# Chunk matrices moved ahead of the last three latent token tiles, and the order of the stores behind them

## The reference, cut to what matters

```python
proj = hn @ w_in                                   # all head groups read columns of it
qkv = silu(causal_depthwise_conv(proj[..., :1536], conv_w))
# gated delta rule, per chunk and head, with the decays of g and beta:
a_low = where(strict, einsum('cd,ed->ce', k_beta, k) * decay, 0)
w = triangular_solve(a_low + eye, k_beta * exp(g));  u = triangular_solve(a_low + eye, v_beta)
# multi-scale pool
o_b = (group_linear(window_means(proj[..., POOL]) - proj[..., POOL])) * pool_scale
# latent attention: q and k from two low-rank latents, normalised per head, rotated
q_c = rotary(rms_norm(rms_norm(proj[..., CQ]) @ w_uq));  kv = rms_norm(proj[..., CKV]) @ w_ukv
x = x + concat[o_a, o_b, o_c] @ w_out
x = x + swiglu(rms_norm(x))
```

## Time and profile before

| | us |
|---|---|
| median of 3 runs | 1263.68 |
| lowest, highest | 1263.26, 1266.42 |
| the profiled execution | 1261.1 |
| its span in the profile | 1259.4 |
| PE busy | 1223.4 (97%) |
| VectorE busy | 826.0 (66%) |
| ScalarE busy | 470.6 (37%) |
| GpSimd busy | 410.7 (33%) |

### The profile page before, as it was taken

One profiled execution on the slowest core, in us unless ns is written; L12 is line 12 of the kernel. 1 busy time (PEld: TensorE's weight loads), 2 busy tenths in 40 slices (PEclk: granted clock), 3 DMA queues, 4 the chain that ended last, 5 costly groups with the idle time before them and its releaser, 6 DMA issues.

```text
span 1259.4 us, 17475 instructions
## 1 busy us (share of the span) xinstructions
PE 1223.4 (97%) x6206; PEld 1022.3 (81%) x6206; DVE 826.0 (66%) x1261; ACT 470.6 (37%) x776; POOL 410.7 (33%) x371
## 2 busy tenths in 40 slices
PE   8999999999798999999999999999999999999998
PEld 7887777887788888888778888888888887888887
DVE  6446777886576676544765656556565589777786
ACT  6312223332334343333544333333333344344342
POOL 6001111441122222102655655665665356100000
PEclk9999999999899999999999999999999999999999
DMA  8311333536732121042325665653667359585544
GB/s 249 119 51 30 113 92 109 164 125 167 251 105 66 56 80 33 1 148 86 119 70 159 206 201 187 214 197 117 201 227 260 92 164 308 174 255 145 175 128 173
DMA packets 190886, 183.17 MB, mean 145 GB/s; under 512 B 19598, under 2 KB 146908, under 8 KB 190812
## 3 DMA queue, kind: packets, MB, share of 16 engines
q1 hardware_dynamic: 190688, 182.16, 45.8%
q10 hardware_dynamic: 124, 0.04, 0.0%
HBM read 124.50 MB, written 56.62 MB: 144 GB/s over the span
## 4 chain that ended last, share of the span: by engine, by line
PE 68%; DVE 17%; issue 5%; POOL 3%; DMA 3%; ACT 3%; SPq 1%; DVEq 0%; ACTq 0%; POOLq 0%
PE ps L2363 30%; PE ps L2368 13%; PE ps L2274 5%; PE ps L2134 5%; PE ps L2010 4%; DVE stage L1594 2%; PE ps L2241 2%; PE ps L2210 1%; PE ps L1986 1%; DVE w_lo L1472 1%; DVE wop_lo L1873 1%; PE ps L2229 1%; DVE stage L1588 1%; POOL mla_sc L964 1%; DVE xop L1857 1%
## 5 line engine op out<-in xcount | busy, mean ns | idle before, releaser
L2363 PE MATMUL ps<-xop,wop_hi 128*128 128x512 f32 x1232 | 379.8, 390 | 1.7 <-ACT snap L1409 0.8
L2363 PEld LDWEIGHTS ps<-xop,wop_hi 128*128 128x128 f32 x1232 | 230.8, 188 | 51.0 <-issue 2.3
L2363 PE MATMUL ps<-xop,wop_lo 128*128 128x512 f32 x616 | 239.7, 389 | 0.0
L2368 PE MATMUL ps<-dop,wop_hi 128*128 128x512 f32 x440 | 136.2, 391 | 2.7 <-DVE x L1955 2.7
L2363 PEld LDWEIGHTS ps<-xop,wop_lo 128*128 128x128 f32 x616 | 115.6, 188 | 24.1
L1873 DVE TENSOR_TENSOR wop_lo<-w_sumS,wop_hi 128x512 fp32r<-128x512 f32 (+1 forms) x104 | 86.7, 836 | 68.6 <-ACT wop_hi L1352 68.6
L1873 DVE TENSOR_TENSOR wop_lo<-w_pair,wop_hi 128x512 fp32r<-128x512 f32 (+1 forms) x76 | 87.4, 1151 | 36.8 <-ACT wop_hi L1352 36.7
L2010 PE MATMUL ps<-act_hi,w_hi 128*128 128x512 f32 x320 | 103.7, 406 | 0.2 <-DVE stage L1594 0.2
L2368 PEld LDWEIGHTS ps<-dop,wop_hi 128*128 128x128 f32 x440 | 82.0, 188 | 22.3 <-DVE wop_lo L1873 3.4
L1955 DVE TENSOR_TENSOR x<-x,ps 128x512 f32<-128x512 f32 x112 | 76.6, 684 | 34.7 <-PE ps L2368 34.7
L2010 PE MATMUL ps<-act_lo,w_hi 128*128 128x512 f32 x320 | 99.1, 391 | 0.0
(11 more groups left out here) (317 smaller groups left out, 2286.9 us busy)
## 6 DMA issues: line engine op xcount, KB each, us to landing
w_pair<-in_w_gate_up SPq DMA_DIRECT2D x44, 512.0 KB, 5.3
hidden<-up SPq DMA_DIRECT2D x22, 512.0 KB, 3.0
wd_rows<-in_w_down SPq DMA_DIRECT2D x22, 512.0 KB, 5.2
raw<-in_w_in SPq DMA_DIRECT2D x21, 512.0 KB, 4.5
wd_raw<-down_sums SPq DMA_DIRECT2D x12, 768.0 KB, 8.4
down_sums<-wd_rows SPq DMA_DIRECT2D x33, 256.0 KB, 2.6
wd_raw<-in_w_down SPq DMA_DIRECT2D x9, 768.0 KB, 7.9
qkv_kept<-qkv_st SPq DMA_DIRECT2D x12, 512.0 KB, 5.3
```

The lines of the kernel that those rows point to most:

```text
L2363: last = pe.matmul(ps[:, bank, :].rearrange("p (t n) -> p t n", n=P), w[:, k, :], a[:, k, :, :], start=(p in ("P1", "P2", "P7") and k == 0 ...
L2368: last = pe.matmul(ps[:, bank, :], w[:, k, :], a[:, k, :], start=(p in ("P1", "P2", "P7") and k == 0 and w is wop_hi[s] and a is hi), stop ...
```

## The change

Four things move.

1. The chunk matrices are made in tiles 12 to 15 instead of 15 to 18 (`M_PREP`), ahead of the last three latent token tiles. Latent tiles 5, 6 and 7 (`BEFORE_PREP` = 5) come behind tiles 16, 17 and 18, their transposes behind 17, 18 and 19. The buffers of the keys move off the latents; `kk_diag` is one buffer instead of two.
2. `base_inverses` follows tile 17's convolution. The splits of tiles 20 and 21 lie behind its steps k = 20 and k = 8, and `mla_means(7)` and `mla_rotate(7)` behind the first of them. GpSimd clears `n_base` earlier.
3. The pool matmuls come behind tile 20 instead of 19.
4. SyncE stores `n_base` before it waits for the last tile. Behind the last tile the moves of the pool results are issued first, ahead of the second chunk's blocks. The loads of `qh` and `kT` come two iterations later.

```diff
-    r = Region(R3_REST)
+    r = Region(R2 + 48 * 1024)
     kch = [r.take(f"kch{b}", [P, GDN_HEADS, P]) for b in range(4)]
...
+    kk_diag = r.take("kk_diag", [P, GDN_HEADS, P])
...
-        M_PREP = M_QKV + 9
+        M_PREP = M_QKV + 6
+        BEFORE_PREP = 5
         PREP_AT = {M_PREP + j: (2 * j, 2 * j + 1) for j in range(TT // 2)}
-        FRONT_AT = {M_FRONT + t: t for t in range(TT)}
-        BACK_AT = {M_FRONT + 1 + t: t for t in range(TT)}
+        FRONT_AT = {M_FRONT + t if t < BEFORE_PREP else M_PREP + 4 + t - BEFORE_PREP: t for t in range(TT)}
+        BACK_AT = {m + 1: t for m, t in FRONT_AT.items()}
...
@@ SyncE @@
                     if c == 0:
-                        sp.wait_ge(mla_front, TT)
...
                 if done == M_GATE - 2:
                     for b in range(2):
                         sp.wait_ge(prep_kept[b], PREP_DMAS * 16 * TT // 2)
+                    sp.wait_ge(raw_used, M_GATE + 1)
                     sp.dma_start(u_base[:, :, :], diag_d.rearrange("q c h i j -> (q c h) i j")).then_inc(u_loaded, 16)
-                if done == M_GATE - 1:
+                if done == M_GATE + 1:
                     for s in range(2):
                         sp.wait_ge(qk_kept[s], 2 * 16 * TT // 2)
...
+                if done == M_GATE - 1:
                     for s in range(2):
                         sp.wait_ge(qkv_kept[s], 16 * QKV_TILES // 2)
                     sp.dma_start(qkvf[0][:, :, :], qkv_d[:, :, 0:P].rearrange("f p n -> p f n")).then_inc(chunk_loaded[0], 16)
+            sp.wait_ge(zeros_kept, 16 * TT)
+            sp.wait_ge(n_solved, 1)
+            for q in range(P // BASE):
+                rows_q = slice(q * BASE, (q + 1) * BASE)
+                sp.dma_start(n_d[rows_q, :, :, rows_q].rearrange("i c h j -> (c h) i j"),
+                             n_base[rows_q, :, :]).then_inc(n_kept, 16)
             sp.wait_ge(gemm_done, IN_ALL)
             sp.wait_ge(mid_act.sem, mid_act.after("pool1"))
...
+            for p in range(2):
+                sp.dma_start(oT[:, :, 4 + p, :], pz[:, p, :].rearrange("p (t n) -> p t n", n=P)).then_inc(pool_moved, 16)
             sp.dma_start(qkvf[1][:, :, :], qkv_d[:, :, P:2 * P].rearrange("f p n -> p f n")).then_inc(chunk_loaded[1], 16)
             for b in range(2):
                 sp.dma_start(E_[b][:, :, :], e_d[b, :, :, :]).then_inc(e_loaded[b], 16)
                 sp.dma_start(A_[b][:, :, :], a_d[b, :, :, :]).then_inc(a_loaded[b], 16)
-            for p in range(2):
-                sp.dma_start(oT[:, :, 4 + p, :], pz[:, p, :].rearrange("p (t n) -> p t n", n=P)).then_inc(pool_moved, 16)
-            sp.wait_ge(zeros_kept, 16 * TT)
-            sp.wait_ge(n_solved, 1)
-            for q in range(P // BASE):
...
@@ GpSimd @@
-            for t in range(TT):
+            def mla_power(t):
                 pool.wait_ge(mla_ms, t + 1)
...
-            pool.wait_ge(mla_front, TT)
+            for t in range(BEFORE_PREP):
+                mla_power(t)
...
+            mla_power(BEFORE_PREP)
+            mla_power(BEFORE_PREP + 1)
+            pool.wait_ge(raw_used, M_GATE + 2)
+            link(pool.memset(n_base[:, :, :], 0.0))
+            pool.memset(n_base[:, :, :].rearrange("p i j -> p (i j)")[:, 0:BASE * BASE:BASE + 1], 1.0).then_inc(filled, 1)
+            mla_power(TT - 1)
...
@@ VectorE @@
-            SPLIT_AT = 24
-
-            def last_split():
-                m = IN_ALL - 1
+            SPLITS_AT = {20: IN_ALL - 2, 8: IN_ALL - 1}
+
+            def split_between(m):
                 dve.wait_ge(gemm_done, m - 1)
                 split_lo(m, m % 2, m % RAW)
+                if m - 2 in FRONT_AT:
+                    mla_means(FRONT_AT[m - 2])
+                    mla_rotate(FRONT_AT[m - 2])
...
-                    if k == SPLIT_AT:
-                        last_split()
...
+                    if k in SPLITS_AT:
+                        split_between(SPLITS_AT[k])
+
+            for m in range(M_QKV, M_GATE):
+                dve.wait_ge(gemm_done, m + 1)
+                split_lo(m + 2, m % 2, (m + 2) % RAW)
+                conv(m)
...
@@ PE @@
+                if t == BEFORE_PREP:
+                    pe.wait_ge(a_ready, TT)
+                    pe.wait_ge(decay_exp, TT)
...
                     if c == 0:
-                        pe.wait_ge(mla_turned, TT)
+                        pe.wait_ge(mla_turned, BEFORE_PREP)
...
-                if m == M_GATE + 1:
-                    pe.wait_ge(a_ready, TT)
-                    pe.wait_ge(decay_exp, TT)
+                if m == M_GATE + 2:
                     pe.wait_ge(pw_loaded, (POOL_GROUPS + 2) * 16)
                     pe.wait_ge(mla_turned, TT)
```

More of the change, by code:

```diff
@@ L149, in hybrid_block @@
     assert r.at <= SBUF_END, r.at - SBUF_END
-    r = Region(R3_REST)
+    r = Region(R2 + 48 * 1024)
     kch = [r.take(f"kch{b}", [P, GDN_HEADS, P]) for b in range(4)]
-    kk_diag = [r.take(f"kk_diag{b}", [P, GDN_HEADS, P]) for b in range(2)]
-    gtg = [r.take(f"gtg{b}", [P, GDN_HEADS, P]) for b in range(2)]
-    assert r.at <= R3_REST + 17 * 1024
+    r = Region(R2 + 60 * 1024)
+    kk_diag = r.take("kk_diag", [P, GDN_HEADS, P])
+    gtg = [r.take("gtg0", [P, GDN_HEADS, P]), Region(R2 + 44 * 1024).take("gtg1", [P, GDN_HEADS, P])]
     r = Region(R3 + 24 * 1024)
@@ L471, in hybrid_block @@
         QKV_ORDER = [4, 5, 6, 7, 0, 1, 2, 3, 8, 9, 10, 11]
-        M_PREP = M_QKV + 9
+        M_PREP = M_QKV + 6
+        BEFORE_PREP = 5
         PREP_AT = {M_PREP + j: (2 * j, 2 * j + 1) for j in range(TT // 2)}
         PREP_DMAS = 2 + P // BASE
-        FRONT_AT = {M_FRONT + t: t for t in range(TT)}
-        BACK_AT = {M_FRONT + 1 + t: t for t in range(TT)}
+        FRONT_AT = {M_FRONT + t if t < BEFORE_PREP else M_PREP + 4 + t - BEFORE_PREP: t for t in range(TT)}
+        BACK_AT = {m + 1: t for m, t in FRONT_AT.items()}
+        assert max(FRONT_AT) == M_GATE
         PRODUCTS = ("P1", "P2", "P6", "P7", "P5", "P3", "P4")
@@ L690, in _ @@
                 sp.dma_start(A_[b][:, :, :], a_d[b, :, :, :]).then_inc(a_loaded[b], 16)
-            for p in range(2):
-                sp.dma_start(oT[:, :, 4 + p, :], pz[:, p, :].rearrange("p (t n) -> p t n", n=P)).then_inc(pool_moved, 16)
-            sp.wait_ge(zeros_kept, 16 * TT)
-            sp.wait_ge(n_solved, 1)
-            for q in range(P // BASE):
-                rows_q = slice(q * BASE, (q + 1) * BASE)
-                sp.dma_start(n_d[rows_q, :, :, rows_q].rearrange("i c h j -> (c h) i j"),
-                             n_base[rows_q, :, :]).then_inc(n_kept, 16)
             sp.wait_ge(n_kept, 16 * P // BASE)
@@ L989, in _ @@
             pool.wait_ge(mask_rows, 2)
-            pool.wait_ge(raw_used, M_GATE + 2)
-            link(pool.memset(n_base[:, :, :], 0.0))
-            pool.memset(n_base[:, :, :].rearrange("p i j -> p (i j)")[:, 0:BASE * BASE:BASE + 1], 1.0).then_inc(filled, 1)
             for c_ in gg:
@@ L1649, in key_means @@
                     dve.wait_ge(key_len, c - 1)
-                link(dve.tensor_tensor(kk_diag[b][:, :, :], heads_view(ps[:, 6 + b, :]), heads_of(ident), ALU.mult))
-                link(dve.tensor_reduce(k_ss[b][:, 0, :], kk_diag[b][:, :, :], axis=AX.X, op=ALU.add))
+                link(dve.tensor_tensor(kk_diag[:, :, :], heads_view(ps[:, 6 + b, :]), heads_of(ident), ALU.mult))
+                link(dve.tensor_reduce(k_ss[b][:, 0, :], kk_diag[:, :, :], axis=AX.X, op=ALU.add))
                 dve.tensor_scalar(k_ss[b][:, 0, :], k_ss[b][:, 0, :], EPS, None, ALU.add).then_inc(key_ss, 1)
@@ L1687, in base_inverses @@
                     done += 2
-                    if k == SPLIT_AT:
-                        last_split()
-            for m in range(M_QKV, IN_ALL):
-                if m < M_GATE or m + 3 < IN_ALL:
-                    dve.wait_ge(gemm_done, m + 1)
-                if m + 3 < IN_ALL:
-                    split_lo(m + 2, m % 2, (m + 2) % RAW)
-                if m < M_GATE:
-                    conv(m)
+                    if k in SPLITS_AT:
[4 more added lines that the diff above has]
+                conv(m)
                 if m + 1 in PREP_AT:
```

## The result

| | before | after |
|---|---|---|
| median (runs) | 1265.05 (4) | 1278.86 (4) |
| lowest, highest | 1263.26, 1268.02 | 1276.00, 1279.42 |
| the profiled execution, its span | 1261.1, 1259.4 | 1278.75, 1277.0 |
| mean granted clock of its span | 0.996 | 0.988 |

The changed kernel is slower: the ratio is 1.0101, with an interval of 1.0083 to 1.0119, which is 0.0101 x 1265.05 = 12.8 us. The forecast was 7.3 us slower and 1271.0, and its range ended at 1275.5. So the direction was right and the size was not. A profile shows one execution only: of 66 executions of the kernel before that ran beside the experiments, four had a mean clock as high as its profile's 0.996, and their mean is 0.992. The profile after is like its runs, all four of which are at 0.988 or 0.989. That is why the two spans differ by 17.6 us, more than the ratio says.

A forecast was written before the change was run, and what follows sets the result against it. PE was taken as full in the projection stage, with VectorE keeping up by 0.06 us. 6.3 us there plus 1.0 us behind the last tile gave 7.3 us slower, 1271.0 us; range 1264 to 1275.5.

The forecast's parts named there:

- The debt of VectorE: Projection stage: VectorE falls behind in chunk-matrix iterations (16.07 us against 13.88); moved earlier, later tiles make PE wait; 6.3 us later.
- The four waits: PE's waits for VectorE before tile 17 and at the transposes behind tiles 17, 18 and 19: 1.1, 1.4, 0, 3.4 us.
- GpSimd's clearing: Clearing of `n_base` beside VectorE's latent work of tile 17: bounded by nothing to 1.2 us, taken as nothing.
- The blocks behind the pool results: Behind the last tile: the second chunk's blocks land 8.4 us after the last matmul instead of 5.1, 3.3 us later.
- Faster: Rival, chance 0.08: the early solve outweighs the waits, first exponential at 7.0 us behind the last matmul, time 1259.0.
- The clock falls as well: Rival, chance 0.15: the 3.4 us wait at tile 19 halves PE's clock for 3.4 or 6.8 us; time 1273 to 1275.
- the later exponential: Behind the last tile: first exponential starts 10.3 us after the last matmul instead of 8.6, a wait 1.8 us longer.
- the transition: Behind the last tile: the 1.8 us longer wait less 0.8 us gained on `w_out`, together 1.0 us later.
- The gain of `w_out`: Behind the last tile: `w_out` loaded some 5 us earlier removes ScalarE's 2.53 us wait; counted as 0.8 us gained.
- The early solve: Solve ends 11 us before the last matmul instead of 6.6 us behind it, so the blocks' landing decides the first exponential.

The follow-up runs named there:

- e1: The changed kernel with the split of tile 20 and latent tile 7's work behind solve step k = 25 instead of 20: 1273.31 us, ratio 1.0061.
- e11: e7 with the last two convolution taps of tile 14 cut to one column each, so less VectorE work: 1262.43 us, ratio 0.9970.
- e2: The changed kernel with the second chunk's blocks, E and A issued ahead of the pool results again: 1271.70 us, ratio 1.0057.
- e4: The kernel before, with only the pool results issued ahead of the second chunk's blocks: 1268.93 us, ratio 1.0025.
- e5: The changed kernel with 14 extra matmuls of 512 columns on PE in the wait behind tile 19: 1276.20 us, ratio 1.0066.
- e6: The kernel before, with the 48 one-column matmuls that sum the latents' squares spread over tile 6: 1262.66 us, ratio 0.9964.
- e7: e3 with the one-column sums of the latents spread over tile 6: 1265.06 us, ratio 0.9982.
- e3: The changed kernel with the edits of e1 and e2 together: 1269.33 us, ratio 1.0025.
- e10: e7 with 4 and 5 extra matmuls of 128 columns ahead of PE's waits for the second chunk's blocks and first exponential: 1261.39 us, ratio 0.9969.

## Why the prediction was right in direction and short in size

**The debt of VectorE: right.** "In the kernel before, this debt is never called in" was the step on which the sign hung. The four waits came within 0.2 us each (1.1, 1.4, 0, 3.4 forecast). e1 takes the last away by the order of the solve, e11 shrinks the others by giving VectorE time.

**GpSimd's clearing: taken at nothing, some 0.5 us too little.** Two instructions of 128x4 took 0.81 and 0.68 us beside it instead of 0.23 and 0.22; they overlap, and what follows them starts 0.5 us later. The bound of 1.2 us held. The clearing wasn't run by itself, so what it adds to PE's waits is not shown.

**The blocks behind the pool results: right, by 0.7 us short.** They land at 9.1 us, not 8.4. The issue of the blocks, 1.30 us long, itself starts 1.45 us after the first issue of the pool results; the prediction counted bytes and not issues. With the order of before and the early solve the exponential starts at 7.1 us (e2), where the rival "Faster" had 7.0.

The sums of the prediction come out to 0.1 us. One label is off: the rows at 188.78 and 202.72 are the ends of tiles 12 and 13, not 11 and 13; the 13.94 us between them stand.

**The step that failed is the clock.** The sum held no term for it in two places. Over all executions the change's mean clock is 0.98825, the 66 of before have 0.9922. By the estimate used at e4 that is 15.0 us lost against 9.8, so some 5.2 of the 12.8 us are clock. The 7.6 us that are left are close to the forecast of 7.3, which had none in it.

- *Behind tile 19.* "The clock falls as well" had a chance of 0.15, with 3.4 us for 6.8 us at the lower level. That is near the size measured (2.9 us in the window at 295.7, between e1 and e5); for the prediction's own time that makes 1274.4. What spoke against it was that the fall ahead of 318.7 followed one-column matmuls and that here PE does dense ones on both sides of the wait. The runs show that this is no protection. The Trainium skill, "TensorE: Matmul & The Clock Gate", section "Why this matters for your kernels", has the rule that a long idle gap between bursts of matmuls puts the clock back to its lower level; the trace agrees in the changed kernel's profile, and not in that of e2, where a gap of 3.16 us left it at 1.00. By that rule the rival would have been the likeliest, at 1272.7, still 6 us short.
- *Behind the last tile.* The prediction priced the later exponential at its 1.8 us and the transition at 1.0 us in all. The wait for the blocks is 5.0 us instead of 1.0, and the low clock is 10.2 + 3.4 us instead of 6.8 (10.2 + 6.8 in e4). How much of that the wait makes is open, since e6 has 10.2 + 3.4 without it; by the mean clocks of e4 it is some 1.3 us. Where the low clock is the same, 13.6 us, the rest of the span is 951.4 to 951.8 us with the pool results first (the change, e1, e5) and 948.7 with the blocks first (e7), so some 3 us are the order itself. In the profiles the transition costs 4.5 us; e4, the order of the loads alone, costs 3.2; taking it back gives 4.5 (e3 against e1) to 5.6 (e2 against the change, part of it clock at tile 19). No rival had it.

**The gain of `w_out`: the wait went, the time did not.** 0.8 us were counted. The wait of 2.53 us is gone, and no profile shows the 0.8 as a shorter end.

**The early solve.** Freed of the wait for the row maximum, the exponential starts 1.5 to 1.7 us sooner in e2 and e3, and yet e3's rest of the span is 1.2 us longer than before's. The two profiles differ in the clock: behind the last tile e3 has 6.8 + 3.4 us at the low level, before 6.8. Where that is equal, 13.6 us in both e7 and e6, the rest of the span is 948.7 us with the early solve and 949.1 with the late one: 0.4 us gained, in one profile each. The stage waits that it brings are 2.6 us. At no point did the early solve earn more than it cost: the best kernel with it (e10) and the kernel before with spread sums (e6) can't be told apart.

**The sum, made again with the measured terms:** waits in the stage 5.7, clock behind tile 19 2.9, order of the loads 3.2 (e4): 11.8 us, against 12.8 by the ratio and 13.8 by the medians. The clock behind tile 19 falls in some executions only, so its mean can be less than 2.9. The four mean clocks of the change, 0.988 and 0.989, against 0.991 and 0.992 in e5 suggest that it fell in most of them; the times don't show at which place. The 3.6 us at 88 us belong to neither kernel in particular. Not run on their own were the pool matmuls behind tile 20, the moved buffers and the later loads of `qh` and `kT`; no wait for any of them stands among PE's waits.

## What to carry to other kernels

Where PE is full, an edit that only moves work can do no more than keep it so: add up the helper engine's time per iteration, and where it has no slack (here 0.06 us), look for the iteration in which its debt is called in. Price a wait of PE with the clock behind it: here 3.2 us of waiting cost 5.1 us by the ratios (6.1 where the clock fell), and a wait of 5.0 in place of 1.0 us behind the last tile cost 3.2 to 5.6. Behind a barrier, issue first what PE waits for first, and put work that nobody awaits (here the pool results) behind it.

## What the runs showed of the hardware

- Executions of one program differ in the clock: e7's twelve had mean clocks from 0.994 to 0.999. A gap of 3.2 us between dense matmuls brought it to 1.2 GHz for 6.8 us in the change's profile and left it alone in e2's.
- Every stretch at 1.2 GHz in the 13 profiles was 3.4, 6.8 or 10.2 us long, but for the one that the end of the span cuts off.
- Matmuls of one column keep PE busy in the records and lose the clock nevertheless: with 48 of them, 5.45 us and no idle time, came 3.4 us at 0.50 behind them before, and 10.2 us at 0.52 in the change, from 1.8 us after their start. Spread between dense matmuls they cost nothing of it (e6).
- Matmuls whose result nobody reads hold the clock: 14 of 512 columns through a wait of 3.3 us (e5), 4 and 5 of 128 columns (8 and 10 in the trace) in the two waits behind the last tile (e10).
- Two of VectorE's smallest instructions took 0.81 and 0.68 us beside GpSimd's clearing of a tile, against 0.23 and 0.22 without it; they ended within 0.1 us of the end of the clearing.
